# Rotary embedding in a two-layer decoder step: the exchange of head halves by four transfers inside SBUF instead of a permutation matmul

## The reference, cut to what matters

```python
def rope(x, pos):
    ...
    cos = jnp.cos(ang)[:, None, :]
    sin = jnp.sin(ang)[:, None, :]
    xf = x.astype(F32)
    x1, x2 = xf[..., : hd // 2], xf[..., hd // 2:]
    return jnp.concatenate([x1 * cos - x2 * sin, x2 * cos + x1 * sin], axis=-1).astype(x.dtype)

def decoder_layer(x, pos, lw, st):
    ...
    q = rope(rmsnorm(zq.reshape(B, T, SWA_HEADS, SWA_HEAD_DIM), q_norm), pos)
    k = rope(rmsnorm(zk.reshape(B, T, SWA_KV_HEADS, SWA_HEAD_DIM), k_norm), pos)
```

## Time and profile before

| | |
|---|---|
| median of 3 runs | 1057.27 us (1057.12 to 1058.95) |
| the profiled execution | 1057.55 us, span 1055.7 us |
| busy: PE, DVE, ACT, POOL | 96%, 66%, 47%, 17% of the span |
| mean granted clock of PE | 0.979 of full speed |
| data moved | 161.87 MB, mean 153 GB/s |
| PE in the chain that ended last | 79% |

### The profile page before, as it was taken

How to read it: one execution, slowest core, us unless ns; L and a number is a source line. 1 busy time by engine, 2 the same in 40 slices (tenths; PEclk the granted TensorE clock), 3 DMA queues, 4 the chain that set the end, 5 groups by cost and what they waited for, 6 DMA issues and landing times.

```text
span 1055.7 us, 18186 instructions
## 1 busy us (share of the span) xinstructions
PE 1010.8 (96%) x7342; PEld 976.8 (93%) x7342; DVE 697.5 (66%) x943; ACT 501.2 (47%) x740; POOL 179.9 (17%) x113
## 2 busy tenths in 40 slices
PE   6999998979999999999999999798899999999998
PEld 6989998969799999999998999798888999999998
DVE  6678776664887555555757787757558865555556
ACT  6428562236255444444554377332552554535354
POOL 0154021225430000000002441305055100000000
PEclk9999998989999999999999999999799999999999
DMA  7554542323365555555564553432334756555552
GB/s 274 178 185 137 183 150 80 101 80 92 121 249 174 164 161 170 162 165 160 170 216 132 175 202 102 132 107 73 100 100 127 271 161 176 162 161 161 173 162 84
DMA packets 43680, 161.87 MB, mean 153 GB/s; under 512 B 5120, under 2 KB 6400, under 8 KB 43040
## 3 DMA queue, kind: packets, MB, share of 16 engines
q1 hardware_dynamic: 42512, 151.73, 45.9%
q0 software_dynamic: 1104, 9.24, 2.2%
HBM read 152.69 MB, written 10.29 MB: 154 GB/s over the span
## 4 chain that ended last, share of the span: by engine, by line
PE 79%; DVE 12%; issue 4%; ACT 3%; POOL 1%; DMA 0%; DVEq 0%; ACTq 0%; POOLq 0%
PE pz L398 70%; PE pm L398 9%; DVE w_lo L949 3%; DVE arena L1149 2%; POOL arena L1438 1%; ACT w_hi L717 1%; DVE arena L1150 1%; DVE arena L1165 1%; DVE arena L1235 1%; PE pm L527 0%; DVE small L1124 0%; ACT a_hi L736 0%; DVE arena L1180 0%; ACT h_hi L926 0%; DVE arena L1199 0%
## 5 line engine op out<-in xcount | busy, mean ns | idle before, releaser
L398 PE MATMUL pz<-a_hi,w_hi 128*128 128x288 f32 x1376 | 418.3, 304 | 11.8 <-DVE w_lo L957 8.3
L949 DVE TENSOR_TENSOR w_lo<-raw,w_hi 128x1024 fp32r<-128x1024 f32 x267 | 351.4, 1318 | 92.8 <-ACT w_hi L717 92.5
L398 PE MATMUL pz<-a_lo,w_hi 128*128 128x288 f32 x1376 | 409.5, 298 | 0.0
L398 PE MATMUL pz<-a_hi,w_lo 128*128 128x288 f32 x1376 | 408.4, 297 | 0.0
L717 ACT ACTIVATE w_hi<-raw 128x1024 fp32r<-128x1024 f32 x267 | 279.5, 1051 | 193.4 <-PE pz L398 189.5
L398 PEld LDWEIGHTS pz<-a_hi,w_hi 128*128 128x128 f32 x1376 | 262.1, 190 | 15.6 <-issue 10.4
L398 PEld LDWEIGHTS pz<-a_lo,w_hi 128*128 128x128 f32 x1376 | 262.5, 191 | 1.2 <-issue 0.8
L398 PEld LDWEIGHTS pz<-a_hi,w_lo 128*128 128x128 f32 x1376 | 262.6, 191 | 0.0
L398 PE MATMUL pz<-h_hi,w_hi 128*128 128x288 f32 x768 | 230.0, 300 | 2.8 <-DVE h_lo L1244 2.8
L398 PE MATMUL pz<-h_lo,w_hi 128*128 128x288 f32 x768 | 227.2, 296 | 0.0
L398 PE MATMUL pz<-h_hi,w_lo 128*128 128x288 f32 x768 | 226.4, 295 | 0.0
(11 more groups left out here) (171 smaller groups left out, 728.9 us busy)
## 6 DMA issues: line engine op xcount, KB each, us to landing
raw<-in_w SPq DMA_DIRECT2D x268, 512.0 KB, 3.6
arena<-in_s SPq DMA_DIRECT2D x2, 2048.0 KB, 9.0
out_ss_out<-arena POOLq DMA_DIRECT2D x2, 2048.0 KB, 9.7
out_u_out<-arena POOLq DMA_DIRECT2D x2, 864.0 KB, 7.4
arena<-in_kcT SPq DMA_DIRECT2D x2, 512.0 KB, 6.0
arena<-in_vc SPq DMA_DIRECT2D x2, 512.0 KB, 7.4
out_kc_out<-in_kc_kept POOLq DMA_DIRECT2D x2, 496.0 KB, 10.2
out_vc_out<-in_vc_kept POOLq DMA_DIRECT2D x2, 496.0 KB, 11.1
```

Of the source, the lines that this page charges most:

```text
L398: return nc.tensor.matmul(out, a, b, start=start, stop=stop, **kw)
L949: tt(w_lo[:, r], raw[:, r], f(w_hi[:, r]), ALU.subtract).then_inc(s["w_lo"], 1)
```

## The change

The permutation matrix and its three matmuls go. At the place where POOL has waited for the norm, it issues four transfers from `qk` to `sin_t`, each of 32 partitions (half a head) by 1440 elements, which swap the two halves of each head. The sine product is now made in place on `sin_t` after the transfers have landed, at unit 10 instead of unit 7 of DVE's list, directly ahead of the add, which reads `sin_t` in SBUF instead of PSUM. The sign moves into the sine table, which is made on the host.

```diff
@@ _constants @@
-    perm = np.zeros((P, P))
-    for i in range(P):
-        if i % HD < HD // 2:
-            perm[i + HD // 2, i] = -1.0
-        else:
-            perm[i - HD // 2, i] = 1.0
-    put("perm", perm)
...
-    return np.ascontiguousarray(np.concatenate(cols, 1)), np.concatenate([np.cos(ang), np.sin(ang)], 1)
+    return np.ascontiguousarray(np.concatenate(cols, 1)), np.concatenate([np.cos(ang), np.where(p % HD < HD // 2, -1, 1)[:, None] * np.sin(ang)], 1).astype(np.float32)
@@ tensor: attention @@
-                if u == 9:
-                    pe.wait_ge(s["qk_sin"], l + 1)
-                    for i in range(3):
-                        last = mm(PM[i][:, 0:480], c("perm"), sin_t[:, i * 480:(i + 1) * 480])
-                    last.then_inc(s["qk_rot"], 1)
@@ vector: attention @@
                     dve.wait_ge(s["qk_norm"], 2 * l + 2)
+                if u == 10:
                     dve.wait_ge(s["cos_sin_landed"], 16 * (l + 1))
-                    tt(sin_t.rearrange("p (j t) -> p j t", j=5), qk.rearrange("p (j t) -> p j t", j=5), bc(sin, 5),
+                    dve.wait_ge(s["qk_rot"], 64 * (l + 1))
+                    tt(sin_t.rearrange("p (j t) -> p j t", j=5), sin_t.rearrange("p (j t) -> p j t", j=5), bc(sin, 5),
                        ALU.mult).then_inc(s["qk_sin"], 1)
-                if u == 10:
-                    dve.wait_ge(s["qk_rot"], l + 1)
                     dve.wait_ge(s["qk_cos"], l + 1)
-                    b3 = lambda a: a.rearrange("p (b n) -> p b n", b=3)
-                    tt(b3(qk), b3(qk_rs), pm[:, 0:3, 0:480], ALU.add).then_inc(s["qk_rope"], 1)
+                    dve.wait_ge(s["qk_sin"], l + 1)
+                    tt(qk, qk_rs, sin_t, ALU.add).then_inc(s["qk_rope"], 1)
@@ gpsimd @@
                 pool.wait_ge(s["qk_norm"], 2 * l + 2)
+                half = HD // 2
+                for o in range(0, P, half):
+                    i_ = o + half if o % HD == 0 else o - half
+                    pool.dma_start(sin_t[o:o + half], qk[i_:i_ + half]).then_inc(s["qk_rot"], 16)
                 pool.wait_ge(s["cos_sin_landed"], 16 * (l + 1))
```

## The result

| | before | after |
|---|---|---|
| median of 10 runs each | 1058.49 us | 1062.95 us |
| the profiled execution | 1057.55 us, span 1055.7 | 1061.75 us, span 1060.0 |
| mean granted clock | 0.979 | 0.974 |

The account below looks back on a forecast made before the run. PE was taken to bound the kernel, with no slack around the rotary step. Layer 0 +3.65 us (+0.25, and 3.4 for half clock) and layer 1 -1.1 gave +2.55: 1059.8 us, range 1053.2 to 1064.5.

Parts of the forecast that it names:

- the transfers are late in both layers: Rival, ahead of DVE's sine product: 32-partition transfers land at 54.7, clock falls in layer 1 too; 1065 us, chance 0.15.
- the configuration costs nothing: Rival, on POOL in layer 0: the configuration only sets a pointer; -3.65 us in total, 1053.6 us, chance 0.28.
- The POOL configuration, the step that decides: POOL, layer 0, before the cosine product: MODIFY_POOL_CONFIG comes onto the path, taken at 4.9 us, bounds nothing to 7.7.
- I take landing in time: Before DVE's sine product: last transfer, issued at 47.0, lands at 49.4 to 52.7; DVE wants it at 51.8 at the earliest.
- Four issues of 0.55 us: POOL, ahead of the cosine product: four transfer issues move its start from 45.35 to 47.55.
- Mutual exclusion of split and cosine product: DVE two-SBUF-input and POOL tensor instructions do not overlap; the split of unit 12 ends 1.07 us after the product.
- PE idle, then half clock: PE before layer 0's first scores: idle for 3.75 us, then clock at half, 3.4 us of work lost.
- The score-read wait of 1.1 us: PE in layer 0, waiting for score reads behind a DVE split held by POOL: the 1.1 us goes away.
- The sum: Both layers: layer 0 +0.25 + 3.4 = +3.65 us, layer 1 -1.1 us, together +2.55 us.
- third rival: Late transfers in both layers: layer 1 at +4.05 us instead of -1.1, layer 0 as forecast; 1065 us, chance 0.15.

Follow-up runs that it names:

- the kernel with an early configuration: Changed kernel plus a 16-column POOL product at the very start, so the configuration instruction runs there; 1063.70 us in a single run.
- the kernel without exchange: Changed kernel without the four transfers and the wait for them, sine product reading queries and keys unswapped; 1055.25 us, ratio 0.9959 to the kernel before.
- the kernel with the held load: Changed kernel, but SP issues the load of unit 15 only once the transfers have landed; 1056.71 us, ratio 0.9975 to the kernel before.
- the kernel with fewer bytes: Changed kernel with POOL's four transfers cut to 576 of 1440 columns, the sine product done in two instructions; 1054.81 us in a single run.

## Why the prediction was right, and where it was not

The time came out in the range and on the side forecast, 1062.95 against 1059.8. In the main that is luck. For the two layers +3.65 and -1.1 us were forecast, and +2.71 and +2.43 came. The story behind the time was mostly another one: the rival "the transfers are late in both layers" joined with "the configuration costs nothing".

- **The POOL configuration, the step that decides.** This is the step that failed. It took 4.9 us for the price, by the mask load as the nearest row; the trace and the kernel with an early configuration show 0.1. Its own 11 ns were the nearer row.
- **"I take landing in time".** This failed as well, and it is the actual cause. The bounds 2.4 to 5.7 us from issue did not hold the fourth transfer (6.5 and 6.4). The reason given, a POOL queue that is empty until then, looked at the queue and not at what else the DMA engines carry. The change itself brings the collision about: it takes the sine product from in front of the split of unit 11, which ends 4.1 us earlier and sends the load of unit 15 into the transfers. The forecast had that split at 45.7 and did not ask what its end triggers. The Trainium skill (DMA: Bandwidth & Descriptors, Issuing engines are not separate DMA queues) says that the queues run on the same 16 engines and interleave. The runs agree: with that load out of the way, the landing took 3.6 us on POOL's queue and 3.7 on SP's; beside it, both the load and the transfers were slower.
- **Four issues of 0.55 us.** Right: 2.10 us. In layer 0 they began 0.6 us after the norm instead of at once, so the product started at 48.17 instead of 47.55.
- **Mutual exclusion of split and cosine product.** Right: the split of unit 12 ended 1.09 us after it (1.07 forecast). It makes the 2.1 us of issues reach PE by way of DVE.
- **PE idle, then half clock.** Right in kind: a wait of PE is followed by a stretch at half clock, 3.4 us lost in each layer, 3.4 taken. But it struck in both layers, where one was forecast, after 3.0 and 2.4 us of idle, where 3.75 was forecast; and the clock fell 1.7 and 1.5 us after PE had restarted, while in the earlier trace rows it fell as PE stood still. That the size agrees is partly chance, since the single run with the early configuration lost 5.1 us in layer 0 after 3.3 us of idle.
- **The score-read wait of 1.1 us.** Gone in layer 0, but not for the reason forecast, that unit 12 meets POOL's L1386 instead of L1387. Here unit 12 ran at half clock, and its split met L1379, which is the L1387 of before. In the kernel without exchange the clock held and unit 12 did meet the counterpart of L1386 (60.75 to 63.81); its split was held all the same, from 62.20 to 64.89, and 0.7 us of PE's wait was left in layer 0:

```profile
PE pm L391 <- DVE arena L1013: 0.7, 2, 0.6
```

  So the earlier scores were worth 0.4 us of that term there; in the changed kernel the slower PE hid the whole of it.
- **The sum.** Layer 0: +0.71 at the scores, -1.1 for that wait, and about 3.1 from the slower clock give the +2.71 at unit 14 (forecast +3.65). Layer 1: scores where they were once the 1.46 us of layer 0 are taken off, -0.4 and about 2.9 from the clock: +2.43 (forecast -1.1, third rival +4.05). Together 5.1; the span grew by 4.3. Between the layers, 2.71 had shrunk to 1.46. Half-clock stretches that the change doesn't touch moved there: before, two near 160 and 219 us and a short one near 304 cost 11.95 us (1 less the granted clock, summed over windows of 1 us), after, two near 165 and 219 cost 10.25, which is 1.7 us less.

## What to carry to other kernels

A transfer that replaces arithmetic must be costed with everything that the DMA engines carry in those microseconds, and the change may move that too: for each instruction that becomes earlier, ask which load its end sets off. Where a second engine issues the transfers, count what stands behind the issues on it: two microseconds on POOL reached PE by way of POOL's product and DVE's split. And a wait of PE is not priced by its own length: here 3.0 us of idle moved the scores by 0.7 us, and the half clock behind it cost some 3 more, which useless matmuls in the gap won back.

## What was not expected of the hardware

- Idle length alone did not decide whether the clock fell: 1.7 us in front of the scores was followed by half clock in the kernel with the held load, 1.8 us in the kernel with fewer bytes was not (one profiled execution of each).
- An issue of this shape took SP 0.65 us (2.59 for four), more than POOL (2.10), while a load of 512 KB took SP 0.33.
- Three matmuls of no use in each layer made the kernel 5.3 us faster.
